# A gather ring of four row buffers instead of six, and a residual stream that stays in place

## The chip, the cores and the metric

The kernel runs on one core of a Trainium2 chip. The core has TensorE (PE, matrix products), VectorE (DVE), ScalarE (ACT), GpSimd (POOL) and SyncE (SP), which share an on-chip memory, SBUF, of 128 partitions; matrix products land in a second memory, PSUM, here one tensor named `bank`. Sixteen DMA engines move data between HBM and SBUF; an engine of the core only issues such a transfer and goes on. Engines and transfers are kept in step by semaphores. The metric is the device time of one execution in microseconds (us), lower is better.

## What is computed

Two transformer-like blocks run one after the other on 256 rows of width 2048. The change lies in the last part of the second block, a feed-forward layer that picks experts: for each of the 256 rows (`n`) it forms 8 x 16 = 128 indices `e` into two tables of 16384 rows of 2048 float32 numbers each, takes the dot product of the row with the 128 chosen rows of the first table, weighs them, and sums the rows of the second table with these weights.

```python
def peer_ffn(h, wq, keys, u_tab, v_tab):
    ...
    def block(args):
        xb, eb, gb = args
        a = jnp.einsum('nd,nhkd->nhk', xb, jnp.take(u_tab, eb, axis=0))
        w = (gb * jax.nn.gelu(a.astype(jnp.float32))).astype(xb.dtype)
        return jnp.einsum('nhk,nhkd->nd', w, jnp.take(v_tab, eb, axis=0))
...
        x_lat = x_lat + m_lat[5] * peer_ffn(hf, peer_wq[l], peer_keys[l], peer_u[l], peer_v[l])
...
    return rmsnorm(x_lat, norm_final)
```

`x_lat` is the residual stream. It is made before the feed-forward layer and is read again only when the layer's result is added to it.

## The kernel before

Each engine has a program of its own that runs in the written order; nothing reorders it. The stages that matter come one after the other:

**The query product (`wq_pe`, `wq_act`, `wq_dve`).** 64 steps; for each, SP loads weights into a ring `raw`, ACT rounds them into `w_hi` (L529), DVE takes the rest `w_lo` (L533), PE multiplies (L542 to L544). Late in it ACT also issues, in `store_parts_act`, three stores of the normalised rows (`hf_rows`, 1 MB each, L2182), a load of a small table `count128` (L2183; the trace calls it `count_sb`) and a store of the residual stream `x` to HBM (`x_rows`, 2 MB, L2184). In between DVE already picks the best keys.

**The choice (`choose_dve`).** DVE forms the indices of the first 128 rows. Its work for the other 128 rows is cut into pieces (`choose_later_dve`) which stand between the dot products of the next stage.

**The gather (`experts_*`), 256 rows.** For row `n`, POOL issues one indirect DMA (L2494) that brings the 128 chosen table rows, 128 x 2048 float32 = 1 MB, into a slot of the ring, one table row on each partition. PE spreads row `n` of the input over all partitions into `bank` (L2516), in two halves. DVE multiplies and sums each half of 1024 columns against the slot (L2582; each is a long instruction followed by a short read of the sum). ACT turns the sums into weights and PE places them (L2524). The ring has six slots: four in `u_ring`, 32 KB on each partition in the place of the weight buffers, and two in `u_more`, 16 KB on each partition in the place of `x`. That is why `x` has been stored. The gather for row `n` waits until DVE has read both halves of row `n - RING`, which held the same slot:

```python
                if n >= RING:
                    pool.wait_ge(halves_read, read(n - RING))
```

The gather for row 128 also waits for `idx_ready`, the indices of the second half. Eight groups of 32 input rows are loaded by SP into `row_ring` (L2504), each as three DMAs of 128 KB; it has two places, so a group is loaded about one group ahead.

**The values (`values_*`).** The second table is streamed in 128 blocks of 1 MB (`v_raw`, L2627). ACT and DVE split each (L2652, L2679), PE multiplies (L2761 to L2763). The first two of the four `v_raw` buffers lie in the places of `u_ring` slots 2 and 3 and are loaded once rows 254 and 255 have been read. After the first four loads SP issues the load of `x` back from `x_rows` (2 MB, L2630). DVE waits for it (`x_back`, L2681) before the last four blocks, where the result is added to `x` (L2712).

Of the kernel before, what the change touches and what calls it, by code (L numbers as in the profile page):

```python
# [28 lines left out]
PH, PK, NK = 8, 16, 128  # L29
RING = 6  # L30
BATCH = 32
# [51 lines left out]
def bass_hybrid_stack_kernel(nc, A, out):  # L83
    ctx = ExitStack()
    with ctx:
# [132 lines left out]
        hf_rows = nc.dram_tensor("hf_rows", (3, S, D), BF16, kind="Internal").ap()  # L218
        x_rows = nc.dram_tensor("x_rows", (S, D), F32, kind="Internal").ap()
        key_s = [at(f"key_s{t}", [P, 16, NK], H_AT + 8192 + t * 8192) for t in range(T)]  # L220
# [37 lines left out]
        u_ring = at("u_ring", [P, 4, D], WS_AT)  # L258
        u_more = at("u_more", [P, 2, D], X_AT)
        placed_w = [at(f"placed_w{t}", [P, NK, P], o) for t, o in ((0, H_AT), (1, XT_AT))]  # L260
# [43 lines left out]
        u_landed = [sem(f"u_landed{i}") for i in range(RING)]  # L304
        x_saved, x_back = sem("x_saved"), sem("x_back")
        v_landed = [sem(f"v_landed{i}") for i in range(4)]
# [1872 lines left out]
        def store_parts_act(act):  # L2179
            act.wait_ge(part_low, NG)  # L2180
            for i in range(3):
                act.dma_start(hf_rows[i].rearrange("(t p) d -> p t d", p=P), parts[:, :, i, :]).then_inc(hf_stored, 16)  # L2182
            act.dma_start(count128[:, :], A["count128"]).then_inc(keys_landed, 16)  # L2183
            act.dma_start(x_rows.rearrange("(t p) d -> p t d", p=P), x[:, :, :]).then_inc(x_saved, 16)  # L2184

# [292 lines left out]
        def u_slot(n):  # L2478

            return u_ring[:, n % RING, :] if n % RING < 4 else u_more[:, n % RING - 4, :]  # L2480

# [4 lines left out]
        def experts_pool(pool):  # L2486
            pool.wait_ge(rings_free, 1)
            pool.wait_ge(x_saved, 16)
            for n in range(S):
                if n % P == 0:  # L2490
                    pool.wait_ge(idx_ready, n // P + 1)
                if n >= RING:
                    pool.wait_ge(halves_read, read(n - RING))
                pool.indirect_dma_start(u_slot(n), None, A["peer_u_2"][0],  # L2494
                                        bass.IndirectOffsetOnAxis(ap=idx[:, n:n + 1], axis=0)).then_inc(u_landed[n % RING], 16)

# [118 lines left out]
        def values_sp(sp):  # L2615
            table = A["peer_v_2"][0].rearrange("(b p) d -> b p d", p=P)

            def four(m, first):
                for j in range(4):
                    b = 4 * m + j  # L2620
                    if not first:
                        sp.wait_ge(values_split, PRE + 4 * b - 12)
                    elif j < 2:
                        sp.wait_ge(halves_read, 2 * PRE + 2 * (S - 1 + j))
                    elif j == 2:
                        sp.wait_ge(weights_taken, PRE + S // 4)
                    sp.dma_start(v_raw[j][:, :], table[bass.ds(b, 1)].rearrange("o p d -> p (o d)")).then_inc(v_landed[j], 16)  # L2627
            four(0, True)
            sp.wait_ge(x_saved, 16)
            sp.dma_start(x[:, :, :], x_rows.rearrange("(t p) d -> p t d", p=P)).then_inc(x_back, 16)  # L2630
            with sp.Fori(0, NK // 4 - 1) as i:
                four(i + 1, False)
            sp.dma_start(last_w[:, :], A["norm_final_2"].partition_broadcast(P)).then_inc(aux_landed, 16)
# [32 lines left out]
        def values_dve(dve):  # L2666
# [13 lines left out]
            passes_of_blocks(dve, four)  # L2680
            dve.wait_ge(x_back, 16)  # L2681
            for j in range(4):
# [238 lines left out]
```

## Time and profile before

| | us |
|---|---|
| median of 3 runs | 3220.5 |
| lowest and highest of them | 3214.74 and 3224.41 |
| the profiled execution, its own time | 3225.26 |
| its span, from first to last instruction | 3223.5 |
| query product and choice up to the first gather | to 1809.7 |
| gather stage, first issue to last dot product | 1809.7 to 2497.4 |
| values and last norm | 2497.4 to 3223.5 |

The rows further down come from the profiled execution. Times in them are microseconds from the start of the span. "Idle before" is the time in which an engine did nothing before an instruction, with what ended it. "To landing" runs from the issue of a DMA to its completion. ACTq and SPq are the sequencers of ACT and SP: an issue of a DMA occupies ACT's program for the time shown, though it is not counted as busy time of the engine.

### The profile page before, as it was taken

The numbers are of one execution on the slowest core, as the hardware profiler recorded it, in microseconds if no ns is written. First come the engines' busy times: TensorE is split into PE (matmuls) and PEld (weight loads), VectorE is DVE, ScalarE is ACT, GpSimd is POOL, SyncE is SP. The second block draws the span as 40 slices with busy tenths as digits, with TensorE's granted clock in tenths as the row PEclk, the third lists the DMA queues.
The fourth block names the chain that finished last, engine by engine and source line by source line (L and its number), as shares of the span: only waits on it lengthen the run. The fifth ranks groups of instructions, "written<-read, shape, count | busy, mean of one in ns | idle before, by whom it ended". The sixth has DMA issues, their size and how long they took to land.

```text
span 3223.5 us, 40241 instructions
## 1 busy us (share of the span) xinstructions
PE 2993.8 (93%) x12354; PEld 2174.8 (67%) x12354; DVE 2394.0 (74%) x4372; ACT 1882.3 (58%) x4171; POOL 319.0 (10%) x380
## 2 busy tenths in 40 slices
PE   8999999999999999988889599889999999999997
PEld 6777878887787877767667233333333788888886
DVE  6787776787767657876857899989999555555556
ACT  5555545555556665445454487678878555555555
POOL 1000000000000000000000233333333000000001
PEclk9999999999999999997999555555555999999999
DMA  7666666776666557970655599989999655555554
GB/s 254 209 203 198 217 224 224 247 236 229 227 234 234 176 170 235 336 284 7 237 172 181 214 411 412 368 344 415 417 416 387 241 194 192 187 194 192 187 194 143
DMA packets 213920, 792.95 MB, mean 246 GB/s; under 512 B 17378, under 2 KB 18098, under 8 KB 151170
## 3 DMA queue, kind: packets, MB, share of 16 engines
q1 hardware_dynamic: 158752, 408.99, 38.4%
q0 software_dynamic: 51344, 370.53, 29.5%
q10 hardware_dynamic: 3668, 11.53, 1.0%
q8 instruction: 76, 1.25, 0.2%
q14 instruction: 80, 0.66, 0.1%
HBM read 783.64 MB, written 7.34 MB: 245 GB/s over the span
## 4 chain that ended last, share of the span: by engine, by line
PE 57%; DVE 21%; DMA 12%; ACT 5%; issue 2%; DVEq 2%; ACTq 1%; SPq 0%
PE bank L542 10%; PE bank L544 10%; PE bank L543 10%; DMA u_ring<-in_peer_u,idx 9%; DVE u_ring L2582 7%; PE bank L2762 7%; PE bank L2761 7%; PE bank L2763 7%; DVE u_more L2582 3%; DVE w_lo L533 3%; DVE acc L597 2%; DMA raw<-in_w_in 2%; ACT w_hi L529 2%; ACT prob L924 1%; PE bank L902 1%
## 5 line engine op out<-in xcount | busy, mean ns | idle before, releaser
L529 ACT ACTIVATE w_hi<-raw 128x512 fp32r<-128x512 f32 x1008 | 621.5, 630 | 664.9 <-PE bank L544 586.8
L533 DVE TENSOR_TENSOR w_lo<-raw,w_hi 128x512 fp32r<-128x512 f32 x1008 | 667.3, 692 | 341.3 <-ACT w_hi L529 336.8
L542 PE MATMUL bank<-w_hi,xt_hi 128*128 128x512 f32 x1632 | 661.0, 405 | 42.9 <-DVE w_lo L533 42.5
L544 PE MATMUL bank<-w_hi,xt_lo 128*128 128x512 f32 x1632 | 639.3, 392 | 0.0
L543 PE MATMUL bank<-w_lo,xt_hi 128*128 128x512 f32 x1632 | 639.2, 392 | 0.0
L2516 PE MATMUL bank<-row_ring,one_row 96*128 96x512 bf16 x1024 | 528.0, 619 | 72.6 <-DVE act_in L2582 38.3
L2679 DVE TENSOR_TENSOR w_lo<-v_raw,w_hi 128x512 fp32r<-128x512 f32 x496 | 343.1, 692 | 283.3 <-ACT w_hi L2652 283.2
L2652 ACT ACTIVATE w_hi<-v_raw 128x512 fp32r<-128x512 f32 x496 | 313.2, 632 | 318.0 <-PE bank L2763 318.0
L2582 DVE CUSTOM_DVE_ANT_0 u_ring<-u_ring,bank 128x1024 f32<-128x1024 f32 x344 | 405.7, 1217 | 39.9 <-DMA u_ring<-in_peer_u,idx 28.5
L542 PEld LDWEIGHTS bank<-w_hi,xt_hi 128*128 128x128 f32 x1632 | 308.1, 189 | 130.0 <-DVE w_lo L533 54.8
L2761 PE MATMUL bank<-w_hi,vw_hi 128*128 128x512 f32 x992 | 390.1, 393 | 2.7 <-DVE w_lo L2679 2.7
L2762 PE MATMUL bank<-w_lo,vw_hi 128*128 128x512 f32 x992 | 391.8, 395 | 0.0
L2763 PE MATMUL bank<-w_hi,vw_lo 128*128 128x512 f32 x992 | 385.9, 389 | 0.0
L544 PEld LDWEIGHTS bank<-w_hi,xt_lo 128*128 128x128 f32 x1632 | 308.0, 189 | 66.6
L543 PEld LDWEIGHTS bank<-w_lo,xt_hi 128*128 128x128 f32 x1632 | 308.4, 189 | 58.6
L2516 PEld LDWEIGHTS bank<-row_ring,one_row 96*128 96x128 bf16 x1024 | 68.6, 111 | 356.3 <-DVE act_half L2582 255.9
L597 DVE SCALAR_TENSOR_TENSOR acc<-ada_ring,c_col,acc 128x2048 f32<-128x2048 f32 x122 | 286.9, 2351 | 16.9 <-DMA ada_ring<-in_ada_w 5.0
L2524 PEld LDWEIGHTS bank<-hot_side,hot_side 128*128 128x128 f32 x512 | 171.1, 335 | 94.7 <-issue 69.6
L2761 PEld LDWEIGHTS bank<-w_hi,vw_hi 128*128 128x128 f32 x992 | 186.9, 188 | 46.7 <-DVE vw_lo L2674 2.9
L2763 PEld LDWEIGHTS bank<-w_hi,vw_lo 128*128 128x128 f32 x992 | 186.8, 188 | 41.9
L2762 PEld LDWEIGHTS bank<-w_lo,vw_hi 128*128 128x128 f32 x992 | 187.2, 189 | 37.2
L2494 POOL DMA_INDIRECT u_ring<-in_peer_u,idx x172 | 162.9, 947 | 486.7 <-DVE act_half L2582 275.5
(450 smaller groups left out, 3501.2 us busy)
## 6 DMA issues: line engine op xcount, KB each, us to landing
v_raw<-in_peer_v SPq DMA_DIRECT2D x128, 1024.0 KB, 4.8
ada_ring<-in_ada_w POOLq DMA_DIRECT2D x96, 1024.0 KB, 5.9
raw<-in_w_in_ab SPq DMA_DIRECT2D x128, 512.0 KB, 4.3
raw<-in_w_in_c SPq DMA_DIRECT2D x128, 512.0 KB, 4.5
raw<-in_w_in SPq DMA_DIRECT2D x120, 512.0 KB, 4.5
raw<-in_w_out_ab SPq DMA_DIRECT2D x32, 512.0 KB, 4.5
raw<-in_w_out_c SPq DMA_DIRECT2D x32, 512.0 KB, 5.5
raw<-in_w_out SPq DMA_DIRECT2D x32, 512.0 KB, 6.6
```

The source lines that it names most:

```text
L529: act.activation(w_hi[:, s % WS, :], raw[:, q % RAW, s % KC, :], ACT.Copy).then_inc(hi_ready, 1)
L533: dve.tensor_tensor(w_lo[:, s % WS, :], raw[:, s // KC % RAW, s % KC, :], w_hi[:, s % WS, :].bitcast(F32), ALU.subtract).then_inc(raw_used, 1)
L542: pe.matmul(o, a_hi, b_hi, start=kk == 0, stop=False, skip_group_check=True)
L543: pe.matmul(o, a_hi, b_lo, start=False, stop=False, skip_group_check=True)
L544: last = pe.matmul(o, a_lo, b_hi, start=False, stop=kk == K - 1, skip_group_check=True)
L597: done = dve.scalar_tensor_tensor(o, ada_ring[:, i % 2, :], c_col[:, v, k:k + 1], o, ALU.mult, ALU.add)
L2516: last = pe.matmul(bank[:, 2 * hf + b, :], wide(one_row[0:3 * BATCH, i:i + 1], [3 * BATCH, P]), row_ring[0:3 * BATCH, g % 2, c:c + 512], s ...
L2582: dve.tensor_tensor_reduce(u, u, bank[:, 2 * hf:2 * hf + 2, :].rearrange("p b n -> p (b n)"), 1.0, 0.0, ALU.mult, ALU.add, (act_in, act_ha ...
L2679: dve.tensor_tensor(w_lo[:, c, :], v_raw[j][:, c * N:(c + 1) * N], w_hi[:, c, :].bitcast(F32), ALU.subtract).then_inc(values_split, 1)
L2761: pe.matmul(o, a_hi, w_hi[:, c, :], start=first and j == 0, stop=False, skip_group_check=True)
L2762: pe.matmul(o, a_hi, w_lo[:, c, :], start=False, stop=False, skip_group_check=True)
L2763: last = pe.matmul(o, a_lo, w_hi[:, c, :], start=False, stop=True, skip_group_check=True)
```

## The change

The ring gets four slots, all in `u_ring`. `u_more` goes, so `x` keeps its place: the store (L2184), the load back (L2630), the tensor `x_rows`, the semaphores `x_saved` and `x_back`, and the three waits on them are taken out.

```diff
-RING = 6
+RING = 4
...
-        x_rows = nc.dram_tensor("x_rows", (S, D), F32, kind="Internal").ap()
...
-        u_more = at("u_more", [P, 2, D], X_AT)
...
-        x_saved, x_back = sem("x_saved"), sem("x_back")
...
             act.dma_start(count128[:, :], A["count128"]).then_inc(keys_landed, 16)
-            act.dma_start(x_rows.rearrange("(t p) d -> p t d", p=P), x[:, :, :]).then_inc(x_saved, 16)
...
-            return u_ring[:, n % RING, :] if n % RING < 4 else u_more[:, n % RING - 4, :]
+            return u_ring[:, n % RING, :]
...
             pool.wait_ge(rings_free, 1)
-            pool.wait_ge(x_saved, 16)
...
             four(0, True)
-            sp.wait_ge(x_saved, 16)
-            sp.dma_start(x[:, :, :], x_rows.rearrange("(t p) d -> p t d", p=P)).then_inc(x_back, 16)
...
             passes_of_blocks(dve, four)
-            dve.wait_ge(x_back, 16)
```

The order of the instructions that stay is the same on every engine. On ACT, in the query product, the program before has this, where `hf_rows`, `x_rows` and `count_sb` are what its DMAs move and the names in brackets are semaphores:

```order
L2182 DMA hf_rows<-parts 128x2x2048 [waits part_low]
L2182 DMA hf_rows<-parts 128x2x2048 x2
L2183 DMA count_sb<-in_count 128x128
L2184 DMA x_rows<-x 128x2x2048
L529 ACTIVATE w_hi<-raw 128x512 [waits chunk_multiplied,w_landed1]
L2292 ACTIVATE key_s_169<-bank 128x512 [waits keys_scored]
```

and the changed one this:

```order
L2179 DMA hf_rows<-parts 128x2x2048 [waits part_low]
L2179 DMA hf_rows<-parts 128x2x2048 x2
L2180 DMA count_sb<-in_count 128x128
L526 ACTIVATE w_hi<-raw 128x512 [waits chunk_multiplied,w_landed1]
L2288 ACTIVATE key_s_169<-bank 128x512 [waits keys_scored]
```

One issue is gone, and the rounding of the next weights follows the small load at once. On POOL, where the gathers begin, the program before issues six without a wait for a slot (`halves_read`), in turn to the two parts of the ring:

```order
L2494 DMA u_ring<-in_peer_u,idx 128x2048 [waits idx_ready,x_saved,rings_free]
L2494 DMA u_ring<-in_peer_u,idx 128x2048 x3
L2494 DMA u_more<-in_peer_u,idx 128x2048 x2
L2494 DMA u_ring<-in_peer_u,idx 128x2048 [waits halves_read] x4
L2494 DMA u_more<-in_peer_u,idx 128x2048 [waits halves_read] x2
```

and the changed one issues four, all to the same tensor:

```order
L2489 DMA u_ring<-in_peer_u,idx 128x2048 [waits idx_ready,rings_free]
L2489 DMA u_ring<-in_peer_u,idx 128x2048 x3
L2489 DMA u_ring<-in_peer_u,idx 128x2048 [waits halves_read] x124
L2489 DMA u_ring<-in_peer_u,idx 128x2048 [waits halves_read,idx_ready]
L2489 DMA u_ring<-in_peer_u,idx 128x2048 [waits halves_read] x127
```

From the fifth gather on, each now waits for the row four before it, where it waited for the row six before it.

## Rows read from the trace of the kernel before

**Rows 1.** Busy time by stretch: gathers' first half, second half, a steady piece, the values.
```profile
core 0: us, PE busy (x) PEld busy (x) DVE busy (x) ACT busy (x) POOL busy (x), PEclk, DMA share, GB/s
1817.00:2163.00 346.00, 310.07 (x769) 119.89 (x770) 334.87 (x692) 264.76 (x793) 117.98 (x122) 0.50 0.97 389
2163.00:2497.00 334.00, 304.61 (x766) 119.62 (x765) 303.07 (x511) 264.83 (x800) 119.86 (x128) 0.50 0.99 405
2186.00:2240.00 54.00, 51.70 (x131) 20.25 (x130) 51.57 (x88) 45.04 (x137) 20.18 (x22) 0.50 1.01 421
...
2501.00:3197.00 696.00, 695.61 (x3028) 570.68 (x3029) 407.35 (x764) 370.62 (x761) 0.00 (x0) 1.00 0.56 195
```

**Rows 2.** DVE's waits in the second half: total, times, longest.
```profile
DVE u_ring L2582 <- DMA u_ring<-in_peer_u,idx: 17.1, 14, 5.7
DVE u_more L2582 <- DMA u_more<-in_peer_u,idx: 1.4, 3, 0.8
```

**Rows 3.** Timeline of DVE, steady second half: start, duration, and what.
```profile
2235.12 1.22 DVE L2582 CUSTOM_DVE_ANT_0 u_more<-u_more,bank 128x1024 f32<-128x1024 f32 x1
...
2240.10 1.22 DVE L2582 CUSTOM_DVE_ANT_0 u_ring<-u_ring,bank 128x1024 f32<-128x1024 f32 x1
```

**Rows 4.** Timeline of POOL in the same place, the next gather's issue.
```profile
2242.74 0.94 POOL L2494 DMA_INDIRECT u_ring<-in_peer_u,idx  x1 [1.55 <-DVE act_half L2582]
```

**Rows 5.** Issue to landing of the steady gathers, 2186 to 2240.
```profile
DMA to landing us min/median/max: 12.2/12.2/12.3
```

**Rows 6.** Timeline of DVE at the end of the stage, when all gathers have landed.
```profile
2492.52 1.22 DVE L2582 CUSTOM_DVE_ANT_0 u_ring<-u_ring,bank 128x1024 f32<-128x1024 f32 x1
...
2494.99 1.22 DVE L2582 CUSTOM_DVE_ANT_0 u_ring<-u_ring,bank 128x1024 f32<-128x1024 f32 x1
```

**Rows 7.** Issue to landing of the gather issued at 2163.20, nothing else under way.
```profile
DMA to landing us min/median/max: 5.4/5.4/5.4
```

**Rows 8.** Timeline of POOL in the first half; two issues are left out between.
```profile
2046.43 0.93 POOL L2494 DMA_INDIRECT u_ring<-in_peer_u,idx  x1 [1.69 <-DVE act_half L2582]
...
2054.68 0.93 POOL L2494 DMA_INDIRECT u_more<-in_peer_u,idx  x1 [2.07 <-DVE act_half L2582]
2057.30 0.93 POOL L2494 DMA_INDIRECT u_more<-in_peer_u,idx  x1 [1.69 <-DVE act_half L2582]
```

**Rows 9.** Issue to landing: two issued 2043.8 to 2046.4, two 2054.7 to 2057.3.
```profile
DMA to landing us min/median/max: 8.0/8.0/8.1
...
DMA to landing us min/median/max: 7.3/7.4/7.5
```

**Rows 10.** Timeline of DVE in the first half: the longest wait on a gather.
```profile
1990.92 1.22 DVE L2582 CUSTOM_DVE_ANT_0 u_ring<-u_ring,bank 128x1024 f32<-128x1024 f32 x1 [1.97 <-DMA u_ring<-in_peer_u,idx]
```

**Rows 11.** Row 33, the largest lead before it: its issue, landing time, dot product.
```profile
1891.67 0.93 POOL L2494 DMA_INDIRECT u_ring<-in_peer_u,idx  x1 [1.72 <-DVE act_half L2582]
...
DMA to landing us min/median/max: 9.7/9.7/9.7
...
1904.71 1.22 DVE L2582 CUSTOM_DVE_ANT_0 u_ring<-u_ring,bank 128x1024 f32<-128x1024 f32 x1
```

**Rows 12.** Pieces of the chain of waits in order of time: start, duration, what.
```profile
1758.91 1.30 ACTq L2184
...
1760.31 0.13 ACT w_hi L529
...
1762.46 0.69 DVE w_lo L533
```

**Rows 13.** DVE's waits from 1763.2 to 1808, and one of ACT's from 1762 on.
```profile
DVE idx L2426 <- PE bank L2472: 0.7, 1, 0.7
DVE gate_s L2416 <- ACT gate_f L2462: 0.4, 1, 0.4
...
ACT w_hi L529 <- DMA raw<-in_peer_wq: 2.0, 1, 2.0
```

**Rows 14.** PE's waits in the values stage, from 2502 on.
```profile
PE bank L2761 <- DVE w_lo L2679: 2.7, 1, 2.7
```

## Prediction

> **What bounds the kernel now.** The change touches two places: the end of the query product, where a store goes, and the 256-row gather stage, where the ring shrinks. I read the table of busy time by stretch first [rows 1]. In the gather stage no engine is full in the second half (DVE 303 of 334 us, PE 305, at half clock), but the DMA engines are: a share of 0.99, and 1.01 at 421 GB/s in the steady piece. In the first half DVE, which also does the choice for rows 128 to 255, is busy for 335 of 346 us, and the DMA engines for 0.97. So the second half runs at the pace of the transfers and the first at that of DVE, with the transfers close behind.
>
> The timelines say how close. In the steady piece dot products start at 2235.12 and, two rows later, at 2240.10: 2.49 us a row [rows 3]. Where all gathers have landed, the last two rows start 2.47 us apart [rows 6]. So the transfers allow one row in 2.49 us, DVE with its partners one in 2.47. DVE's waits for a gather in the second half sum to 17.1 + 1.4 us, 5.7 of them at its first row [rows 2]; waits below 0.15 us are not in that list.
>
> How long a gather takes tells little by itself. It takes 12.2 us in the steady piece [rows 5] and 5.4 us with nothing else under way [rows 7]. The 12.2 us is the ring: the dot product at 2240.10 lets POOL issue the next gather into that slot at 2242.74 [rows 3, 4], so a landing is followed by its successor's issue after 2.66 us (the dot product starts 0.02 us after the landing), and 12.25 + 2.66 = 14.9 us is six rows of 2.485 us. Most of the 12.2 us is standing in line behind other gathers. A shorter ring shortens the line first, and costs time only once there is no line left.
>
> **Term 1, the ring in the steady state.** With four slots a gather may take 4 x 2.485 - 2.66 = 7.3 us from issue to landing before the row time grows. It needs 5.4 us alone [rows 7]. That leaves 1.9 us. The row that comes nearest to the new state is in the first half, where DVE is slowed by its pieces of choice: the gather issued at 2046.43 lands 8.1 us later at 2054.5, the one issued at 2054.68 comes 0.2 us after that and finds two more ahead of it, exactly what a ring of four would show, and it lands after 7.5 us; the next, issued at 2057.30, after 7.3 us [rows 8, 9]. Their landings, 2062.2 and 2064.6, are 2.4 us apart. So the engines keep their full pace with a line of two, and the steady state costs 0. Bounds: 0 by these rows; the upper one is the first rival's.
>
> **Term 2, the lead that the ring can save up.** In the first half DVE's average row takes 346 / 127 = 2.72 us, more than the transfers' 2.49, so landings run ahead of DVE until the ring is full, and this lead later absorbs a disturbance such as a group load of input rows (384 KB on the same engines) or one engine that falls behind. Row 33 has the largest lead before the only longer wait of that half: issued 1891.67, landed 9.7 us later at 1901.3, used at 1904.71, a lead of 3.4 us [rows 11]. With four slots the issue comes two rows later, some 2 x 2.6 = 5.2 us, which leaves 13.0 - 5.2 = 7.8 us for a transfer of at least 5.4 to 5.7 us: a lead of 2.1 to 2.4 us. So 1.0 to 1.3 us of lead is lost, and since DVE has run out of lead at 1990.92, where it waits 1.97 us [rows 10], that much arrives in the time: +1.1 us. In the second half there is no lead to lose on the slowest DMA engine, but the faster ones can be ahead by 1.9 us at most, where 12.2 - 5.4 = 6.8 us was allowed; a delay that hits a fast engine may then show. I take +0.5 for it (bounds 0 and, if two or three such delays of about 1 us show, +3). Later in the first half the pieces of choice make DVE's rows 2.6 us and more [rows 8], which refills the lead between group loads; I take nothing there. Term 2: +1.6 us (0 to +4).
>
> **Term 3, the store of x that goes.** ACT issues it at 1758.91 for 1.30 us, and the chain of waits runs through that issue: the next rounding starts at 1760.31, and DVE's w_lo at 1762.46 [rows 12]. From there to 1808 DVE has only two waits, of 0.7 and 0.4 us [rows 13], so it carries any gain on to the first gather. Gain 1.3 us. The lower bound is 0: a little later ACT waits 2.0 us for a block of weights that shares the DMA engines with these stores [rows 13], and if that block landed no earlier, ACT's wait could grow by the 1.3 us won. The upper bound is 1.3 + 2.0 = 3.3 us, if with 2 MB fewer under way that wait goes as well and DVE gains by it. I take -1.3, the issue's own length: DVE does not wait for ACT there now [rows 13], so the block has some room already, and it should land sooner.
>
> **Term 4, the load of x back and the waits.** The load's 2 MB compete with the table blocks at 2500 to 2513. In the whole values stage PE waits once, 2.7 us, for the first split [rows 14], and is busy for all 695.6 us of it [rows 1]; the load is issued after the first four blocks, so that wait was not its doing. Gain 0; its cover is PE, and nothing replaces it. The waits of POOL, SP and DVE on x_saved and x_back go with the two transfers; the store is issued 50 us before the first gather, and none of them ends a wait in these rows. 0. The two v_raw buffers in slots 2 and 3 are freed by rows 254 and 255 in either ring (254 is 2 modulo 4 and modulo 6), so the values start no later.
>
> **Sum.** +1.6 - 1.3 + 0 = +0.3 us on the profiled execution's 3225.3, so 3225.6. That execution lies 4.8 us above the median of the runs; against the median, 3220.5 + 0.3 = 3220.8 us.
>
> **A page against the trace.** The rows show 5.4 us on an idle machine. The Trainium skill (DMA: Bandwidth & Descriptors, section Latency and other measured facts) gives HBM access as 0.2 us on average and 2 us at high load. By it a gather under load would need an estimated 5.4 + 1.8 = 7.2 us, and the 1.9 us in hand would be 0.1: the steady state would still hold, but hardly a lead could be saved, and the sum would be about rival B's +6 in place of +1.6. The landings of 7.3 to 7.5 us at full pace neither contradict it nor need it.
>
> **Rivals.**
> A, slower: the part of a gather that is not standing in line is longer under load than the 5.4 us of the idle one. It decides at 7.3 us. If it is 8.0, the largest typical value with a short line [rows 9], a row takes (8.0 + 2.66) / 4 = 2.67 us, in 127 rows of the second half 0.18 x 127 = +23 us; the first half has 2.72 us a row already and adds perhaps 3. 3220.5 + 26 - 1 = 3245 us. Against it: the two landings 2.4 us apart with a line of two; for it: these are only two rows, and DVE was the slower party there.
> B, the lead matters more: each of the six later group loads costs about 1 us, +6 in place of +1.6, 3225 us. For it: the loads are seen at both waits of some 2 us. Against it: where transfers bound, they are paid already.
> C, the other transfers matter more: -3.3 in place of -1.3, the ring free of charge, and the row 0.015 us shorter in the second half (2 us), as DVE's 2.47 would allow: 3220.5 - 5.3 = 3215 us. Even this is not 0.3%, or 9.7 us, which is about what a measurement of this kernel can tell from no change.
>
> **How the numbers follow.** Forecast 0.55, A 0.14, B 0.17, C 0.10, and 0.04 for a gain that nothing here shows. Within 0.3%: forecast, B and C, 0.82; slower 0.14; faster 0.04. The range takes in B and C with the 5 us by which single runs lie from the median on either side, and the lower part of A (a floor up to 7.6 us, 10 us): 3211 to 3232.
>
> **What would show it.** Right: gathers in the steady second half land after 7.2 to 7.4 us, dot products stay 2.49 us apart, the DMA share stays at 1.0, the first gather is issued at about 1808.4, and the stage from there takes 688 to 692 us (687.7 before). Wrong: landings above 7.4 us with rows above 2.5 us and a DMA share below 0.97 (A); more waits of 1 us or above on a gather in the first half (B); a first gather before 1807.5 (C). The values stage should keep its length; if it doesn't, term 4 is wrong.

## The result, and the profile after

The changed kernel took 3242.07 us (median of 5 runs, 3237.62 to 3256.09) beside 3220.5 of the kernel before (now also 5 runs, the same median): a ratio of 1.007, 95% interval 1.0046 to 1.0094. It is slower by 21.6 us, where I had forecast no change and put the upper end of the range at 3232. (Ratios and intervals here are those on record; they differ by up to 0.0015 from the quotients of the medians beside them.) The profiled execution took 3246.82 us, with a span of 3245.0.

Busy time by stretch, the changed kernel: first half of the gathers, second half, and the values (columns as in [rows 1]).

```profile
1821.00:2176.00 355.00, 312.49 (x769) 120.21 (x770) 335.42 (x692) 265.56 (x792) 120.35 (x124) 0.50 0.98 379
2176.00:2519.00 343.00, 306.13 (x767) 119.77 (x765) 303.01 (x512) 265.62 (x800) 119.88 (x128) 0.50 0.99 395
...
2524.00:3220.00 696.00, 696.00 (x3035) 571.12 (x3036) 408.08 (x765) 370.50 (x760) 1.11 (x1) 1.00 0.55 191
```

Against [rows 1] each engine's work is the same (DVE 335.4 and 303.0 us, before 334.9 and 303.1), the values have kept their length (from the last dot product to the end of the span 726.1 us before and 725.5 now), and both halves of the gathers have grown by 9 us. The DMA share is as high as it was (0.98 and 0.99), but the engines move less: 379 and 395 GB/s in place of 389 and 405. Whoever reads only the share sees almost nothing.

The whole of the stage, from the first gather's issue to the end of the last dot product, was 687.7 us and is 706.1. This execution is a long one: in two other executions with four buffers (the changed kernel once more, and the one with only the ring changed, both below) the stage takes 701.7 and 701.4 us, so the stage has grown by 14 to 18 us. The remaining 3.6 us had come up before: the first gather is issued at 1813.33 in place of 1809.70. That place moves from execution to execution whatever the ring (1808.4 with five buffers, 1815.0 with the ring alone changed, and 1801.3 in the second execution of the changed kernel), so I give it no cause.

DVE's waits by what ended them (total us, times, longest), the changed kernel, first half (1822 to 2176) and then second (2176 to 2520):

```profile
DVE u_ring L2577 <- DMA u_ring<-in_peer_u,idx: 21.1, 19, 8.4
...
DVE u_ring L2577 <- DMA u_ring<-in_peer_u,idx: 28.2, 30, 5.8
```

In the kernel before, the first half (1809 to 2163) has

```profile
DVE u_ring L2582 <- DMA u_ring<-in_peer_u,idx: 11.4, 4, 8.3
```

and the second has [rows 2], 18.5 us in 17 waits. So the change adds no long wait. It adds many, most of them of about 0.3 to 1.3 us, in both halves: 30 in place of 17, and 19 in place of 4.

Between them the ring does what term 1 of the prediction said. Issue to landing of eight gathers in a row, issued from 2213.2 to 2230.6, the changed kernel:

```profile
L2489 POOL DMA_INDIRECT u_ring<-in_peer_u,idx x8: 936/936/939, 2213.2 to 2230.6; - x8
...
DMA to landing us min/median/max: 7.2/7.2/7.3
```

That is the 7.3 us that four buffers allow, and these gathers land 2.48 us apart: full pace, with nothing in hand. Over the whole second half the median from issue to landing is 7.6 us.

**One such wait in both kernels.** About once in 50 us one DMA engine fetches 16 KB of instructions. The DMA engines from 2242 to 2248, the changed kernel (queue, kind: packets, MB, share of the 16 engines; the packet starts at 2244.1):

```profile
q8 instruction: 1, 0.02, 1.1%
```

and DVE's timeline there:

```profile
2246.81 1.22 DVE L2577 CUSTOM_DVE_ANT_0 u_ring<-u_ring,bank 128x1024 f32<-128x1024 f32 x1 [1.28 <-DMA u_ring<-in_peer_u,idx]
```

The fetch took 1.06 us and DVE waits 1.28 us for row 152. The kernel before has the same fetch at 2228.8, from 2227 to 2233:

```profile
q8 instruction: 1, 0.02, 1.1%
```

and no wait of DVE's anywhere from 2180 to 2250; its gathers there all take 12.2 to 12.3 us [rows 5]. With six buffers this delay of one engine reaches nobody; with four it arrives whole. In the stage there are 43 instruction fetches in either kernel, each a single packet, 23.6 us of packets before and 23.0 now.

**A late issue.** Not every delay is a DMA engine's. In either kernel POOL issues three gathers 1.3 to 1.5 us later than usual once their buffer is free, rows 19, 113 and 221 before, rows 19, 113 and 223 now. This is the last of them, now:

```profile
2428.59 0.94 POOL L2489 DMA_INDIRECT u_ring<-in_peer_u,idx  x1 [3.06 <-DVE act_in L2577]
```

The same delays stand in the profiled executions of the experiments below with one depth throughout and no added copies, and they are a test of the depth by itself. With five or six buffers, five executions, DVE waits for none of the three rows. (The two versions with six and then four have the first two of these delays, under six buffers, and no wait either.) With four, also five executions, it waits 0.3 to 1.7 us more than usual for row 113 and 0.5 to 2.0 for row 223. With three it waits for all three, 1.6 to 2.2 us each.

**All the waits, sorted.** For each wait of DVE's for a gather, 0.15 us or more over the usual 0.12 between rows, I looked for what stands next to the landing: a load of input rows, a late issue, an instruction fetch (begun at most 2.5 us before the landing ahead of it), or, with none of these, a wait for the row one turn of the ring earlier. Rows 3 to 127 and 132 to 255, us in total:

```
                      group   late    fetch   one turn   nothing
                      load    issue           earlier    found     sum
six (before)           8.2     0       3.8     0          0        12.0
four (changed)        10.8     3.6     9.8     3.8        2.5      30.5
four (changed again)  11.4     1.9     9.3     2.1        4.1      28.8
```

From six buffers to four the sum grows by 18.5 us, as much as the stage, and in the second execution by 16.8, where the stage grows by 14.0. This says what each wait stands beside, and doesn't prove its cause.

The single packets say how the time is lost. A gathered row is 128 packets of 8 KB, eight for each of the 16 DMA engines. Their mean durations, counted over the packets that start in each half, with the lengths of the halves (issue of gather 0 to dot product 128; dot product 128 to 255):

```
                    first half            second half
                    mean ns   length us   mean ns   length us
six (before)        325.4     358.9       316.6     326.4
five                326.9     357.9       317.3     325.8
four (changed)      336.1     368.5       325.4     335.3
three               354.3     402.3       348.8     373.0
```

The medians are 309 to 313 ns in all of them; what grows is the number of long packets (over 400 ns: 1.7% before, 4.1% changed in the second half). 8.8 ns more for each of 16,220 packets on 16 engines is 8.9 us, and the second half is 8.9 us longer. That the two agree is no proof of a cause: with a DMA share near 1 the packets' durations must fill the time. It says where the time is booked, spread over many long packets, and a long packet is also what an engine shows that has stood idle. The gather for row 128 in the kernel before, with nothing else under way [rows 7], shows this: its first 21 packets, begun from 2164.83 to 2165.34, took 0.38 to 1.06 us, and nearly all of those begun after 2165.8 took 0.309.

### The profile page after: what moved, and what is told of

Read it like the earlier page. It is cut to its first block, busy times and chain, and to the rows that moved or that the text cites. A ratio compares the mean times of both kernels' runs of the same rounds, so it can differ in the third digit from the quotient of the medians.

```text
span 3245.0 us, 40238 instructions
## 1 busy us (share of the span) xinstructions
PE 3003.2 (93%) x12354; PEld 2181.6 (67%) x12354; DVE 2394.1 (74%) x4372; ACT 1883.6 (58%) x4171; POOL 319.5 (10%) x380
## 4 chain that ended last, share of the span: by engine, by line
PE 58%; DVE 18%; DMA 14%; ACT 5%; issue 2%; DVEq 2%; ACTq 1%; POOL 0%; SPq 0%
DMA u_ring<-in_peer_u,idx 12%; PE bank L539 11%; PE bank L541 10%; PE bank L540 10%; DVE u_ring L2577 8%; PE bank L2753 7%; PE bank L2755 7%; PE bank L2754 7%; DVE w_lo L530 3%; DVE acc L594 2%; ACT w_hi L526 2%; ACT prob L921 1%; DMA raw<-in_w_in 1%; PE bank L899 1%; DMA ada_ring<-in_ada_w 0%
## 5 line engine op out<-in xcount | busy, mean ns | idle before, releaser
L2577 DVE CUSTOM_DVE_ANT_0 u_ring<-u_ring,bank 128x1024 f32<-128x1024 f32 x512 | 603.8, 1216 | 64.6 <-DMA u_ring<-in_peer_u,idx 49.3
L2489 POOL DMA_INDIRECT u_ring<-in_peer_u,idx x256 | 244.1, 953 | 643.3 <-DVE act_half L2577 432.1
```

The costliest lines, as they stand in the source:

```text
L2577: dve.tensor_tensor_reduce(u, u, bank[:, 2 * hf:2 * hf + 2, :].rearrange("p b n -> p (b n)"), 1.0, 0.0, ALU.mult, ALU.add, (act_in, act_ha ...
```

## The theories

**H1, the depth.** A buffer is free only when all 16 DMA engines have delivered its row. So the depth of the ring says how far an undelayed engine may run ahead of the one that was delayed last. With six buffers that is up to 12.2 - 5.4 = 6.8 us, and delays on different engines overlap: DVE sees about the sum of the worst engine. With four it is 1.9 us, the others soon have nothing to fetch, and most single delays add up. Since the engines are the bound (2.49 us a row), nothing lost is regained.
**H2**: the loads of the later groups of input rows alone cost more with four buffers (the prediction's rival B). **H3**: the loaded latency has a floor near 7.2 us (rival A in a mild form). **H4**: taking out the store and the load of x costs the time.

The times of the kernel before beside which the runs stood were 3224.05 us (four and five buffers with x stored, three buffers, six and then four), 3224.87 (the loads left out, the thirty copies), 3224.71 (the copies by two issuers, the early step) and 3226.06 (the slower VectorE, the changed kernel again).

## Experiments: how deep, and which part of the change

Four buffers, x still stored and loaded back:

```
-RING = 6
+RING = 4      (the kernel before)
```

> The kernel before with one edit: the gather's ring has four row buffers, and x is still stored and loaded back. H1 (with four buffers each DMA engine can run only about 1.9 us ahead of the one that was disturbed last, so that nearly every single delay of one engine reaches VectorE): the gather stage is as long as in the changed kernel, some 18 us over the 687.7 us of before, and the whole lies near 3243 us (3239 to 3248). If the kept transfers matter (H4): without their removal the stage is short again, near 3222 us.

Measured 3243.37 us, ratio 1.0055 (1.0031 to 1.008). The halves are 367.8 and 331.3 us. The ring alone makes the loss, and H4 falls.

Five buffers:

```
-RING = 6
+RING = 5      (the kernel before)
```

> The kernel before with five row buffers in place of six. A lone gather may now take 5 x 2.485 - 2.66 = 9.8 us before VectorE waits, 2.5 us more than with four, 2.5 us less than with six. H1: most single delays (0.3 to 1.9 us) are covered again, so +2 to +7 us over before, 3222 to 3228 us. If only the floor of the loaded latency counted (H3, 7.3 us needed): 0, 3220 us. If the loss goes evenly with the number of buffers: +9 us, 3230 us.

Measured 3228.45 us, ratio 1.0013 (0.9997 to 1.0028), halves of 357.9 and 325.8 us in the profiled execution, the fastest of its ten (3222.2 us). DVE's waits in its second half:

```profile
DVE u_ring L2582 <- DMA u_ring<-in_peer_u,idx: 15.6, 16, 5.9
DVE u_more L2582 <- DMA u_more<-in_peer_u,idx: 3.4, 4, 2.2
```

19.0 us, as with six (18.5). The median lies just over the 3222 to 3228 that H1 expected. The loss doesn't go evenly with the number of buffers: what the sixth is worth isn't clear of noise (4 us by the medians, an interval of about 0 to 9), the fifth is worth some 15 us by the medians. H3 expected the same here, so this run doesn't tell H1 and H3 apart; the next does.

Three buffers:

```
-RING = 4
+RING = 3      (the changed kernel)
```

> The changed kernel with three row buffers in place of four. The latency of a gather that is alone is 5.4 us, so a row takes at least (5.4 + 2.66)/3 = 2.69 us in place of 2.485: 256 rows x 0.2 us = +52 us over the changed kernel, and every single delay of a DMA engine comes on top. H1: 3295 to 3340 us. H3 (a floor of the loaded latency of 7.2 us whatever is in flight): (7.2 + 2.66)/3 = 3.29 us a row, +205 us, near 3450 us.

Measured 3309.97 us, ratio 1.0247 (1.0218 to 1.0276). Issue to landing of the gathers from 2220 to 2580:

```profile
DMA to landing us min/median/max: 5.4/5.9/8.7
```

and the busy time from 2220 to 2585:

```profile
2220.00:2585.00 365.00, 306.07 (x748) 116.88 (x746) 294.77 (x497) 258.96 (x778) 116.08 (x124) 0.50 0.96 359
```

A gather among others can take as little as 5.4 us, 5.9 at the median. H3 falls (it wanted 3450 us), and with it rival A and the prediction's estimate of 7.2 us for a gather under load, as far as 359 GB/s is load: the steady piece of the kernel before moves 421 [rows 1]. A row takes 373.0 / 127 = 2.94 us, 0.09 over the (5.9 + 2.66) / 3 = 2.85 of the median gather.

Six buffers in the first half, four in the second. The two further buffers lie where the raw scores were, which is free until the weights of the second half are placed:

```
+u_more = at("u_more", [P, 2, D], RAW_AT)
 rows 0 to 127:   buffer n % 6
 rows 128 to 255: buffer (n - 128) % 4
```

> The changed kernel, but rows 0 to 127 go through six row buffers, which lie where the raw scores were and which nothing needs until the expert's weights come; rows 128 to 255 go through four as in the changed kernel. x stays in its place, nothing is stored or loaded back. H1: the first half loses its 9.5 us (361.7 us back to about 352), the second keeps its 9: near 3233 us (3229 to 3236). H2 (only the loads of the later groups of input rows cost): these lie in both halves, the first half gains 3 to 5 us, near 3238 us. H4 (the removal of the transfers costs the time): no gain, near 3242 us.

Measured 3231.19 us, ratio 1.0015 (0.9999 to 1.0031). First half 358.4 us, as with six; second 334.0, as with four. Its waits, first half and second:

```profile
DVE u_ring L2592 <- DMA u_ring<-in_peer_u,idx: 9.9, 4, 8.4
...
DVE u_ring L2592 <- DMA u_ring<-in_peer_u,idx: 27.7, 35, 6.0
```

4 waits and 35, in one kernel, near the 4 of the kernel before and the 30 of the changed one. The loss follows the depth, half by half.

## Experiments: which delays

The six later loads of groups of input rows left out, with four buffers and with six. Rows 64 to 255 are then multiplied with input rows that don't belong to them, so this leaves a part of the computation out:

```
-for g in range(S // BATCH):
+for g in range(2):
```

> The changed kernel without the six later loads of groups of input rows, so that the rows of the later groups are multiplied with what lies in their buffers (this part of the computation is left out). The only planned transfers beside the gathers are gone from the first part of the stage. H2 (the group loads alone make the loss): the kernel falls by 18 us or more, to about 3222 us, and stands no higher than the kernel before without the same loads. H1 (any delay of a single DMA engine): the loads were some 6 to 11 us of it, 3231 to 3236 us, and the distance to the kernel before without them stays 12 to 18 us.

> The kernel before without the six later loads of groups of input rows (this part of the computation is left out). H1: it gains the 6 us that the two loads at rows 162 and 194 cost, and little more: 3212 to 3217 us, 12 to 18 us under the changed kernel without them. H2: the distance to that one falls below 4 us.

Measured 3234.87 and 3218.15 us, ratios 1.002 (1.0003 to 1.0037) and 0.9978 (0.9961 to 0.9994). From gather 0 to dot product 255 the stages are 695.0 us (703.8 with the loads) and 677.2 us (685.3). So the loads cost 8.8 us with four and 8.1 with six. The 703.8 is the long execution, though; two others with four buffers have 699.3 and 699.0, which makes it some 4 us. The distance stays (16.7 us by the medians), within the 12 to 18 that H1 expected; the run with six, 3218.15, lies 1 us over its expected range. H2 and the prediction's rival B fall: the loads don't cost more with four buffers.

The run with four shows something that H1 had not said. DVE's waits for gathers of 0.9 us and more, from 2290 to 2352:

```profile
2295.00 1.22 DVE L2575 CUSTOM_DVE_ANT_0 u_ring<-u_ring,bank 128x1024 f32<-128x1024 f32 x1 [1.39 <-DMA u_ring<-in_peer_u,idx]
2306.06 1.22 DVE L2575 CUSTOM_DVE_ANT_0 u_ring<-u_ring,bank 128x1024 f32<-128x1024 f32 x1 [1.28 <-DMA u_ring<-in_peer_u,idx]
2317.17 1.22 DVE L2575 CUSTOM_DVE_ANT_0 u_ring<-u_ring,bank 128x1024 f32<-128x1024 f32 x1 [1.33 <-DMA u_ring<-in_peer_u,idx]
...
2349.79 1.22 DVE L2575 CUSTOM_DVE_ANT_0 u_ring<-u_ring,bank 128x1024 f32<-128x1024 f32 x1 [0.98 <-DMA u_ring<-in_peer_u,idx]
```

With the two between (1.22 us at 2328.17, 0.91 at 2338.86) these are rows 172, 176, 180, 184, 188 and 192: every fourth, the ring's own period. At row 172 there are two fetches (0.33 us at 2291.9, 1.10 us at 2292.8), at 180 two small ones, at 176, 184, 188 and 192 none at all. A late row frees its buffer late, the next gather into that buffer is issued late (the one at 2297.64 comes 3.76 us after its forerunner in place of 2.47), engines run out of packets meanwhile, and the row is late again. The busy time before and in this piece:

```profile
2280.00:2290.00 10.00, 9.42 (x24) 3.63 (x22) 9.24 (x17) 8.36 (x26) 3.75 (x4) 0.50 1.01 420
2300.00:2320.00 20.00, 17.10 (x43) 6.59 (x43) 16.90 (x29) 14.79 (x46) 6.75 (x8) 0.50 0.96 360
```

420 GB/s and then 360, while the share says 0.96. Such echoes are in the changed kernel too (rows 172, 176, 180 with 1.03, 0.38, 0.34 us; 214, 218, 222 with 1.00, 0.84, 0.26) and not in the kernel before or the one with five buffers. So a part of the loss isn't fetches that no longer overlap, but the same delay paid again. By the lone gather above, an engine that has stood idle also starts again with a long packet, which may be part of the echo. Why the late gather, with 4.6 us in hand at its issue, lands 3.80 us after its forerunner, and not 2.49, I can't say from these rows.

**Delays made on purpose.** Thirty copies of 24.6 KB, each one descriptor, one after every fourth gather from row 139 on, into a scratch tensor (some waits that go with them are left out here):

```
+if n >= P + 8 and n % 4 == 3:
+    e = (n - P) // 4
+    pool.dma_start(spare[e:e + 1, 0:6143], placed_w[0][e:e + 1, ...]).then_inc(extra_stored, 16)
```

> The kernel before with 30 extra transfers added in the second half of the gather stage: before every fourth gather from row 139 on, GpSimd issues one copy of 24.6 KB that is a single descriptor, and so lies on a single DMA engine, another one each time. At the 8 KB in 0.31 us of the gathers' packets each delays one engine by about 0.94 us. Six buffers. H1: an engine may lead by up to 6.8 us, each of the 16 is hit about twice, so VectorE sees about the worst engine's sum of 2 to 4 us: +2 to +6 us over before, 3222 to 3227 us. If GpSimd's issue of the extra copies or the bandwidth is what costs: the same amount as with four buffers.

> The changed kernel with the same 30 extra copies of 24.6 KB, one DMA engine each. Four buffers. H1: the delays of different engines add up, since none may lead by more than about 1.9 us: up to 30 x 0.94 = 28 us, at least 10: 3252 to 3270 us, that is 8 to 24 us more than the same copies cost with six buffers. H2 (delays of single engines are not what costs, only loads on all engines): +2 to +6 us, as with six buffers, 3244 to 3248 us.

Measured 3249.86 us with six, ratio 1.0075 (1.0057 to 1.0093), and 3258.97 with four, ratio 1.0091 (1.0055 to 1.0127). That is 25 us over the kernel before, where I expected 2 to 6, and 17 us over the changed one, inside the expected 3252 to 3270. The expectation for six was wrong, and the trace says why: I had taken it that each copy hits another engine. DVE's first three added waits with six buffers:

```profile
2211.08 1.22 DVE L2589 CUSTOM_DVE_ANT_0 u_ring<-u_ring,bank 128x1024 f32<-128x1024 f32 x1 [0.74 <-DMA u_ring<-in_peer_u,idx]
...
2221.89 1.22 DVE L2589 CUSTOM_DVE_ANT_0 u_more<-u_more,bank 128x1024 f32<-128x1024 f32 x1 [0.98 <-DMA u_more<-in_peer_u,idx]
...
2232.71 1.22 DVE L2589 CUSTOM_DVE_ANT_0 u_ring<-u_ring,bank 128x1024 f32<-128x1024 f32 x1 [1.00 <-DMA u_ring<-in_peer_u,idx]
```

and the marks that the 16 engines leave when they have finished a gather (us before the last one):

```
gather   first    last but two   last but one   last
138      -1.40    -0.88          -0.55          0
150      -2.87    -1.53          -1.41          0
154      -3.82    -2.30          -1.94          0
158      -4.71    -3.20          -2.84          0
```

One engine alone falls behind all the others, by 0.9 us with each copy (a packet of 24.6 KB takes 0.91 to 0.92 us), and never regains it; from row 174 on it stays 4.4 us or more behind the next one. All thirty hit the same engine. Their packets sum to 30 x 0.91 = 27 us, and the second half grows by 21.6 us with six buffers (348.0 for 326.4) and by 19 to 23 with four (354.1 for 335.3 or 331.3). So the pair shows two things other than those it was made for. Delays that always hit the slowest engine cost most of their length at either depth. And the stage has nothing to regain them with, which is H1's second half. By the medians the copies cost less with four buffers (17 us against 25), by the second halves they don't, so I conclude nothing from that difference. H1's main point, delays on different engines, remains untested by this pair.

The same thirty copies, half of them issued by SyncE:

```
-if n >= P + 8 and n % 4 == 3:     (GpSimd)
+if n >= P + 8 and n % 8 == 3:     (GpSimd)
+for n % 8 == 7: sp.wait_ge(half_spread, 2 * PRE + 2 * n); sp.dma_start(spare..., placed_w[0]...)
```

> The kernel before with 30 copies of 24.6 KB added in the second half of the gather stage, 15 of them issued by GpSimd and 15 by SyncE in turn, each one descriptor. In the run in which GpSimd issued all 30, every copy hit the same DMA engine and VectorE lost 0.7 to 0.9 us to each, with six buffers as with four. If SyncE's copies land on another DMA engine, H1 (six buffers let one engine lag while another is delayed) expects only one of the two sums to show, 15 x 0.88 = 13 us over before: near 3237 us. If they land on the same engine, or if the buffers do not separate the engines at all: 23 to 26 us as with one issuer, near 3249 us.

> The changed kernel with the same 30 copies by two issuers. H1 with two different engines: with four buffers an engine may lead by only some 1.9 us, but copies that alternate between two engines keep these two within 0.9 us of each other, so that each pair costs 0.9 to 1.8 us: +13 to +26 us over the changed kernel, 3255 to 3268 us. If the copies of both issuers land on one engine: +17 to +26 us, as with one issuer (3259 us).

Measured 3257.88 us with six, ratio 1.0112 (1.0072 to 1.0153), and 3268.65 with four, ratio 1.0131 (1.0112 to 1.0151). The marks show one engine falling behind again, by both issuers' copies in turn (spread at gather 158 with six buffers: first -4.55, last but one -2.82, last 0). So this pair too couldn't put delays on different engines. It costs 8 and 10 us more than with one issuer, and both times lie above what I expected for copies on one engine (near 3249 and 3259). The extra time lies in the second half (356.6 us for 348.0, and 362.9 for 354.1). It doesn't come from groups of input rows held back behind SyncE's copies: PE waits for none of them there. Its cause stays open.

**A slower VectorE.** One small operation after each row, in both kernels, and the changed kernel once more:

```
+if n < S - 4:
+    dve.tensor_tensor(paused[:, n % 2, :], eye[:, 0:48], eye[:, 0:48], ALU.add)
```

> The kernel before with one more small operation on VectorE after each row of the gather stage (48 columns of a constant added to themselves, some 0.1 us with its start). VectorE's pace per row becomes 2.55 to 2.65 us in place of 2.485, while the DMA engines keep their 8 packets of 0.31 us = 2.49 us a row. H1: a DMA engine that was delayed now regains 0.06 to 0.16 us with every row. The kernel grows by 252 x 0.1 = 25 us (15 to 40), less the few us that delays cost in the second half before: 3238 to 3260 us.

> The changed kernel with the same small operation after each row. H1 (the loss of the shallow ring comes from delays that the DMA engines can't regain, since their pace and VectorE's are the same): with a slower VectorE delays are regained and the distance to the same kernel with six buffers falls from 18 us to 3 to 9 us. If the loss has another cause that goes with each row or each load whatever the pace (a fixed price of the shallow ring): the distance stays 18 us.

> The changed kernel once more, unaltered, beside the two with the slower VectorE: 3242 us (3237 to 3248), 17 to 20 us over the kernel before.

Measured 3235.18 us (1.0031, 1.0019 to 1.0043), 3243.87 (1.0049, 1.0033 to 1.0064) and 3239.52 (1.0052, 1.0028 to 1.0075). Two expectations were missed: with six buffers the operation costs 9 us where I expected 15 to 40, and the changed kernel again is 13.5 us over the kernel before, not 17 to 20. So the loss by the whole times is 13.5 to 21.6 us in three comparisons, by the stage 14 to 18. The distance between four and six falls from 13.5 us to 8.7, at the upper edge of what H1 expected. But the pair's premise was wrong in the second half. There the median row still takes 2.49 and 2.48 us: the operation, 0.20 us in the profile, fits into the time in which DVE waited anyway, and the half with six buffers has 325.8 us, as without it. The distance between the second halves doesn't fall (6.9 us, against 4.9 to 8.9). The operation lengthens the first halves (366.5 us for 358.9, and 375.1 for 368.0), and the distance between these is 8.6 us, near the 9.1 it was. So I take no verdict from it on H1, but it doesn't support it: in the first halves, where the operation did slow DVE, H1 wanted the distance to fall clearly. What it shows is that in the second half DVE isn't the bound, and that this much of its work there is free.

## Experiments: a version that beats both

The largest single wait of the stage, after that for its first row, is in both kernels (5.7 and 5.8 us): gather 128 is issued when dot product 127 is done, because VectorE takes the indices of the second half only then. It takes them five rows earlier:

```
-if n == TURN_AT + 7:
+if n == TURN_AT + 2:
     take_choice_dve(dve, 1)
```

> The kernel before with one edit: VectorE takes the indices of the second choice five rows earlier, before row 123 in place of before row 128. Gather 128, which now is issued when row 127 is done and lands 5.4 us later, can then be issued as soon as its buffer is free, and the 6.7 us and 2.0 us in which VectorE waits for gathers 128 and 129 are gone. -8 us: 3214 to 3218 us beside 3224 of before. If GpSimd's issues or the choice itself are late there (the piece of PE that turns the choice is not done by row 122), VectorE waits inside the step instead, and the gain is 0 to 4 us.

Measured 3216.9 us, ratio 0.9977 (0.9961 to 0.9993), as expected. DVE's waits around row 128, from 2140 to 2180, in the kernel before:

```profile
DVE u_ring L2582 <- DMA u_ring<-in_peer_u,idx: 7.7, 2, 5.7
```

and in this one, where no line names a gather:

```profile
DVE u_ring L2582 <- PE bank L2516: 1.9, 4, 0.9
```

The two waits for gathers 128 and 129 are gone. This is the fastest version that computes everything, 8 us under the kernel before; its gain is between 0.07% and 0.39%.

The same in the changed kernel with six and then four buffers, the four taken in such an order that gather 128 needs the buffer of row 122:

```
-return n % RING if n < P else (n - P) % LATER
+return n % RING if n < P else (n - P + 2) % LATER
```

> The changed kernel with six row buffers for rows 0 to 127, four for rows 128 to 255 (in an order in which gather 128 needs the buffer of row 122, 129 that of 123) and the indices of the second choice taken five rows earlier. x stays in its place. The two gains add up: 3231 us of the kernel with six and then four, less 8 us for the gap at row 128: 3221 to 3225 us, 7 us over the kernel before with the early step alone, since the second half still has four buffers.

Measured 3224.71 us, ratio 0.9992 (0.9979 to 1.0004). So x can stay in its place at no loss, 8 us over the early step with six buffers, as expected. Six buffers throughout with x in its place have no room in the second half, and weren't tried.

## Why the prediction was wrong, point by point

**What bounds the kernel**: right for the second half, and it was the key that I didn't use. That half runs at the pace of the DMA engines; so whatever makes an engine idle there is time, and there is nothing to make it good with. For the first half I had DVE as the bound, and so expected it to be the safe one; it lost as much.

**Term 1, steady state 0**: right. 7.2 to 7.3 us from issue to landing, 2.48 us apart, in the undisturbed pieces. Rival A is refuted by the run with three buffers. What I had wrong is how much of the stage is undisturbed.

**Term 2, the lost lead, +1.6 us (0 to +4)**: the step that failed, by its size. I counted the lead of the slowest engine, as DVE sees it, and allowed "two or three such delays of about 1 us" for the fast ones. Measured: +9.6 us in the first half (358.9 to 368.5; four other executions with four buffers had 367.2 to 369.4, three others with six 358.4 to 358.7) and +5 to +9 in the second (326.4 to 335.3; two other executions with four buffers throughout had 331.3, two with four only there 334.0 and 334.3). The trace of the kernel before would have given a number of delays: 43 instruction fetches of 23.6 us in the stage. An upper end of +23 us from them, in place of +4, would have held the result. In the first half I said that the lead refills between group loads. It does for six buffers: from row 8 on the median row has landed 2.1 us before DVE takes it. With four it is 0.4 us, and 19 waits for 4 is the outcome.

**Term 3, -1.3 us**: right, though the whole times can't show it. In the changed kernel ACT's next rounding begins at 1763.99, 3.7 us later than before, but everything there is later, the stores too. From the issue of the first store of `hf_rows` to the first gather it is 54.6 us before and 54.3 changed, and over all profiled executions of this document 54.5 to 55.8 us (median 55.7) in the eight that store x and 53.1 to 54.3 (median 54.3) in the nine that don't. That is a gain of some 1.4 us.

**Term 4, 0**: right. From the last dot product to the end it is 726.1 us before and 725.5 changed, and PE is busy throughout the 696 us of the values.

**Rivals**: A's time was near (3245) by luck, its mechanism wrong. B had the right place, the lead, and the wrong cause: the loads that hit all engines cost 8.1 us with six buffers and 4 to 9 with four. C fell.

**What would show it**: I had named a DMA share below 0.97 as a sign of A. The share stayed at 0.98 and 0.99, and the GB/s fell. The sign of the loss was in the next column. The stage's length, which I had put at 688 to 692 us, showed it too.

Shown is: the depth alone makes the loss, most of it between five buffers and four, half by half; and delays that hit all engines, or always the slowest one, cost about as much with four as with six. Not shown is H1's main point, that the many single delays are on different engines and that six buffers let them overlap. It rests on rows like the fetch at 2228.8 and 2244.1, not on an experiment of its own. Shown without that is that the same late issue of POOL's, 1.5 us, costs nothing with five or six buffers and 0.3 to 2.0 us with four, so H1 is also too narrow: the depth covers delays of POOL's as it does those of the DMA engines. How the loss divides I know only by what each wait stands beside: of the 18.5 us in the table above 5.9 are beside fetches, 3.8 one turn after an earlier wait, 3.6 at late issues, 2.6 at group loads, and for 2.5 I found nothing.

## What to carry to other kernels

The depth of a ring of DMA buffers isn't settled by the latency of one transfer against the pace of the consumer. Here the 16 engines were the bound, four buffers covered the latency, and four still lost 14 to 18 us where five lost none that is clear of noise. So count the short delays in the trace of the deeper ring (instruction fetches, late issues, group loads), take their sum as the size of what a shallower ring may lose (here fetches of 23.6 us, for a loss of 14 to 18), though not as a strict bound, since a delay can come back each turn, and try one buffer more than the latency asks for. And read GB/s beside the DMA share.

## What the runs showed of the hardware that I had not expected

- Copies of one descriptor (24.6 KB, 0.91 us each) from GpSimd and SyncE alike all went to the same DMA engine of the 16; it fell behind by 0.9 us with each and was never level with the others again in the stage.
- Instruction fetches are packets among those of the gathers: in 688 us 30 of 8 KB (0.31 us) and 13 of 16 KB (1.05 us).
- The DMA share can stay at 0.96 while the engines move 360 GB/s in place of 420: 8 KB packets of 0.31 us are then recorded with up to 2 us. The first 21 packets of a gather with nothing else under way took 0.38 to 1.06 us, those behind them 0.309.
